# Attention of a mixer stage with keys and values expanded per head, head pairs in the two halves of TensorE, and the weights around it loaded earlier

## The chip, the cores and the metric

The kernel runs on one core of one Trainium2 chip. The metric is the device time of one execution in microseconds (us). Engine names are those of the profile: PE is TensorE, DVE is VectorE, ACT is ScalarE, SP is the engine that issues most DMAs.

## The reference

The program is a chain of blocks over 1024 tokens of width 1024. The change is in one of them, a mixer with sparse attention that runs between two feed-forward stages. Cut to what matters:

```
proj = h @ w_in                      # q (8 heads x 64), c (latent, 128), qi, ki, wi (index), z (gate, value)
c = rmsnorm(c)
q_abs = einsum('blhd,hcd->blhc', q, w_uk) * 64 ** -0.5
for each block of 128 queries:
    score = einsum(wi, relu(qi . ki));  score = where(causal, score, -inf)
    sel = top_k(score, 256)                           # the 256 keys that this query may see
    sc = q_abs . c[sel];  p = softmax(sc)             # 8 heads
    out = einsum('bqhc,hcd->bqhd', p @ c[sel], w_uv)
att, gmlp -> concatenated -> @ w_out -> deepnorm with the residual -> layernorm
```

The product q_abs . c equals q . (w_uk^T c), and (p @ c) @ w_uv equals p @ (c @ w_uv); either order may be used.

## The kernel before

The mixer stage (`mixer_stage`) has two parts, each a block of its own with a barrier behind it.

**Part "in_2"** computes `h @ w_in` in 16 tiles of 128 columns, each 48 matmuls of 512 columns in three fp32r products. Around the tiles it computes the index scores, the gated unit (`mix(n)`, eight matmuls whose outputs lie in alternating column halves, L2625) and the first steps of the selection. The threshold of the 256th score is found bit by bit, 64 rounds in all, 32 for blocks 2 to 4 and 32 for blocks 5 to 7. In one round (`rank_round`) DVE counts two blocks (L2498, twice), ACT the third (L2512), and DVE makes the next candidate (L2502, L2504). The table `ROUNDS_AFTER` puts 41 rounds into "in_2"; the other 23 are in the attention part, spread over its first 37 heads.

**Part "attention"** goes over 8 blocks of 128 queries and 8 heads, n = 8 b + h from 0 to 63. Block b sees k = b + 1 tiles of 128 keys. Its prologue transposes c (L2921) and makes q_abs per head (L2929, matmuls over 64 rows, alternating row halves); it waits for w_uk, w_uv and the mask, whose DMAs are issued as the part begins. For each n:

- PE: `score_head`, q_abs . c over 128 rows (L2887), k x 128 columns, into one of two halves of four PSUM banks.
- DVE: `add`, adds mask or selection and takes the row's maximum (L3051), then negates it (L3054).
- ACT: exponential with row sum (L2977).
- PE: k transposes (L2895); ACT copies them to SBUF, up to four tiles a copy (L2964).
- PE, once per pair of heads: `latent`, k matmuls of 256 columns (L2904); ACT copies (L2996); `value`, two matmuls of 64 columns (L2916).

Every engine's order is written out by hand; semaphores count the steps. PE does `score_head(n + 1)` ahead of the transposes of n. Once per block DVE scales the output by the inverse row sums (L3062, L3063), PE transposes it and ACT copies it to `mT`. Between heads DVE turns thresholds into a mask (`select`, L3011 to L3037) as a filler: `take(fill, ...)` runs its pieces up to a budget. `select(b)` must be done before the first head of block b.

After it `combine_stage("out_2", ...)` multiplies by `w_out`. Weights come through a ring of two slots (`Weights`): DMA into `ring_b_raw`, `cut_high` on ACT (L239), `cut_low` on DVE (L242). The part begins with the loads of its first two tiles (`primed` is False), then cuts `mT` in the same way, then multiplies.

Of the kernel before, what the change touches and what calls it, by code (L numbers as in the profile page):

```python
# [8 lines left out]
P = 128  # L9
D = 1024  # L10
KD = D // P
SEQ = 1024
CTX = 256
T = SEQ + CTX
DB = 512
# [9 lines left out]
NEG = -1.0e30  # L25
# [57 lines left out]
def program(nc, A):  # L83
# [18 lines left out]
    with root:  # L102
# [2336 lines left out]
        def mixer_stage(mT, ring, head):  # L2439
# [17 lines left out]
            MIX_AFTER = {13: (0, 1, 2), 14: (3, 4, 5), 15: (6, 7)}  # L2457
            MEAN_BANKS, VAR_BANKS, KV_BANKS = (6, 7), (2, 5), (6, 7)
            ROUNDS_AFTER = {3: 2, 4: 3, 5: 3, 6: 4, 7: 4, 8: 4, 9: 4, 10: 4, 11: 1, 12: 4, 13: 2, 14: 4, 15: 2}
# [4 lines left out]
                     "mix_ready", "a_loaded", "a_ctok", "a_ctok_ready", "a_qabs", "a_qabs_ready", "a_scored", "a_added",  # L2464
                     "rank_asked", "rank_told", "causal_added", "a_exp", "a_transposed", "a_turned", "a_latent", "a_latcopy", "a_value", "a_rescaled")
            S = {n: sem("att_" + n).h for n in names}

            with ExitStack() as mixer:
# [12 lines left out]
                links = []  # L2481
# [9 lines left out]
                def rank_round(link, dve, n):  # L2491

# [3 lines left out]
                    for i, b in enumerate(groups[g][:2]):  # L2496
                        w = (b + 1) * P
                        link(nc.vector.tensor_scalar(junk[:, 0:w], scores(b), cand[:, g, i:i + 1], float(TOPK - signed),  # L2498
                                                     ALU.is_ge, ALU.add, accum_out=found[:, g, i:i + 1]))
                    dve.wait_ge(S["rank_told"], n + 1)  # L2500
# [24 lines left out]
                with ExitStack() as ctx:  # L2525
# [29 lines left out]
                    with nc.Block("in_2") as block:  # L2555
                        @block.sync
                        def _(sp):
# [5 lines left out]
                            for m in range(n_tiles):  # L2563
                                if m >= 2:
                                    ring.load(sp, m // 2, m % 2, A["w_in"][tiles[m][1]])
                                if m == 2:
# [3 lines left out]
                                        .then_inc(S["mx_loaded"], 16)  # L2570

# [169 lines left out]
                        def _(dve):  # L2741
# [32 lines left out]
                            for m, _ in enumerate(steps):  # L2774
# [41 lines left out]
                                for _ in range(ROUNDS_AFTER.get(m, 0)):  # L2816
                                    rank_round(link, dve, ranked_here)
                                    ranked_here += 1
# [7 lines left out]
                qabs = sb(mixer, "at_qabs", [P, NH, SEQ])  # L2826
                ctok = sb(mixer, "at_ctok", [P, NQ, P])
                def uk(n):
                    return xT[:, n // 2, SEQ + n % 2 * P:SEQ + n % 2 * P + P]

                uv = sb(mixer, "at_uv", [P, NH, 64])
# [5 lines left out]
                sm = ring.raw[:, :].rearrange("p s k t -> p s (k t)")  # L2837
                pr = sb(mixer, "at_pr", [P, 2, SEQ])
                pT = sb(mixer, "at_pT", [P, 2, NQ, 2, P])
                mx = sb(mixer, "at_mx", [P, 2])  # L2840
                nmx = sb(mixer, "at_nmx", [P, 2])
                rs = sb(mixer, "at_rs", [P, 2, NH])
                lat = sb(mixer, "at_lat", [P, 2, 2, P])
                osb = sb(mixer, "att_rescaled_o", [P, 2, DB])
                N = NQ * NH
                PAIRS = N // 2
                STEPS = N + 7

                pieces, upto, out_at = [], {}, {}
                for n in range(STEPS):  # L2850
# [463 lines left out]
```

## Time and profile before

| | |
|---|---|
| median of 3 runs | 4023.18 us (4019.23 to 4026.61) |
| the profiled execution | 4014.95 us, its span 4013.2 us |
| granted TensorE clock, mean share of full | 0.958 |
| PE busy over the span | 3536.3 us (88%) |
| DVE, ACT busy over the span | 1917.4 us (48%), 1155.6 us (29%) |
| the attention part in the span | from 2862.8 to 3133.8 us |

A row of the view by windows gives the stretch, its length, then for PE, its weight loads, DVE, ACT and POOL the busy time and the count of instructions, then the granted clock (1.00 is 2.4 GHz, 0.50 is 1.2 GHz), DMA share and GB/s. A row of the timeline gives start, length, engine, line, operation, out<-in, shapes and count, and in brackets the idle time before it and what ended it. A row of the waits gives who waited for whom, the total, the times and the longest. A row of the groups gives busy time and mean ns of one, then idle time before. An fp32 matmul has two records in the trace.

### The profile page before, as it was taken

Reading aid. Unit: us, or ns where it says so; the run is one execution under the profiler, and the core shown is the slowest. Engines: PE = TensorE matmul, PEld = TensorE weight load, DVE = VectorE, ACT = ScalarE, POOL = GpSimd, SP = SyncE. Lnnn points to the kernel's source line nnn. Section 1 sums busy time; section 2 is a strip of 40 time slices with the busy share of each in tenths; the row PEclk is TensorE's granted clock in tenths of the full one; section 3 lists DMA queues with packets and bytes.
Section 4 is the critical chain, followed back from the end, with each engine's and each line's share of the span. In section 5 each row is a group of like instructions: output and inputs, shape, how many; then the busy total and the mean of one; then the engine's idle time right before and its main releaser. Section 6 shows DMA issues by size and latency. Waiting matters only on the chain. (4 is left out here: it accounts for less than half of the span.)

```text
span 4013.2 us, 67402 instructions
## 1 busy us (share of the span) xinstructions
PE 3536.3 (88%) x30218; PEld 2843.2 (71%) x30218; DVE 1917.4 (48%) x2775; ACT 1155.6 (29%) x1730; POOL 74.3 (2%) x85
## 2 busy tenths in 40 slices
PE   2999889998667777789999999999678889999997
PEld 1888678886256677647888888667456768888885
DVE  7555565643565565465222222657784552222226
ACT  2111231223434433333111111345364331111113
POOL 0000000000000000000000000110000020000000
PEclk9999999999789999989999999999799999999999
DMA  4233311223732222042111111210000211111112
GB/s 176 98 120 104 134 42 48 95 100 108 254 96 58 54 77 77 21 158 68 48 48 48 52 49 44 71 45 32 6 1 1 74 53 48 48 52 48 48 44 93
DMA packets 141796, 284.68 MB, mean 71 GB/s; under 512 B 8148, under 2 KB 81236, under 8 KB 141252
## 3 DMA queue, kind: packets, MB, share of 16 engines
q1 hardware_dynamic: 126212, 250.80, 19.4%
q10 hardware_dynamic: 15296, 29.57, 2.1%
q8 instruction: 238, 3.90, 0.4%
q14 instruction: 50, 0.41, 0.0%
HBM read 234.42 MB, written 45.65 MB: 70 GB/s over the span
## 5 line engine op out<-in xcount | busy, mean ns | idle before, releaser
L242 DVE TENSOR_TENSOR ring_b_wl<-ring_b_raw,ring_b_wh 128x1024 fp32r<-128x1024 f32 (+1 forms) x200 | 236.2, 1181 | 1115.2 <-ACT ring_b_wh L239 1115.2
L274 PE MATMUL PS<-ffn_x_high,ring_b_wh 128*128 128x512 f32 x1408 | 552.1, 392 | 11.0 <-DVE ffn_x_low L524 7.2
L276 PE MATMUL PS<-ffn_x_high,ring_b_wl 128*128 128x512 f32 x1408 | 549.8, 391 | 0.0
L275 PE MATMUL PS<-ffn_x_low,ring_b_wh 128*128 128x512 f32 x1408 | 549.8, 390 | 0.0
L239 ACT ACTIVATE ring_b_wh<-ring_b_raw 128x1024 fp32r<-128x1024 f32 (+1 forms) x200 | 204.6, 1025 | 1189.2 <-PE PS L276 1173.5
L274 PEld LDWEIGHTS PS<-ffn_x_high,ring_b_wh 128*128 128x128 f32 x1408 | 265.3, 188 | 72.8 <-DVE ffn_x_low L524 10.3
L276 PEld LDWEIGHTS PS<-ffn_x_high,ring_b_wl 128*128 128x128 f32 x1408 | 265.2, 188 | 55.2
L275 PEld LDWEIGHTS PS<-ffn_x_low,ring_b_wh 128*128 128x128 f32 x1408 | 265.4, 188 | 54.5 <-issue 0.2
L274 PE MATMUL PS<-ffn_hid_high,ring_b_wh 128*128 128x512 f32 x704 | 275.5, 391 | 2.6 <-DVE ring_b_wl L242 2.6
L276 PE MATMUL PS<-ffn_hid_high,ring_b_wl 128*128 128x512 f32 x704 | 274.4, 390 | 0.0
L275 PE MATMUL PS<-ffn_hid_low,ring_b_wh 128*128 128x512 f32 x704 | 274.3, 390 | 0.0
L242 DVE TENSOR_TENSOR ring_a_wl<-ring_a_raw,ring_a_wh 128x1024 fp32r<-128x1024 f32 x72 | 88.1, 1225 | 338.1 <-ACT ring_a_wh L239 337.8
L274 PE MATMUL PS<-in_o_high,ring_a_wh 128*128 128x512 f32 (+1 forms) x608 | 231.2, 380 | 10.9 <-DVE in_o_low L524 5.7
L239 ACT ACTIVATE ring_a_wh<-ring_a_raw 128x1024 fp32r<-128x1024 f32 x72 | 76.1, 1058 | 569.0 <-PE PS L276 545.0
L275 PE MATMUL PS<-in_o_low,ring_a_wh 128*128 128x512 f32 (+1 forms) x608 | 228.8, 376 | 0.0
L276 PE MATMUL PS<-in_o_high,ring_a_wl 128*128 128x512 f32 (+1 forms) x608 | 228.6, 376 | 0.0
L274 PE MATMUL PS<-in_e_high,ring_a_wh 128*128 128x512 f32 (+1 forms) x576 | 208.8, 363 | 14.4 <-DVE in_e_low L524 13.0
L275 PE MATMUL PS<-in_e_low,ring_a_wh 128*128 128x512 f32 (+1 forms) x576 | 205.0, 356 | 0.0
L276 PE MATMUL PS<-in_e_high,ring_a_wl 128*128 128x512 f32 (+1 forms) x576 | 204.9, 356 | 0.0
L274 PEld LDWEIGHTS PS<-ffn_hid_high,ring_b_wh 128*128 128x128 f32 x704 | 132.2, 188 | 32.2 <-DVE ring_b_wl L242 4.6
L275 PEld LDWEIGHTS PS<-ffn_hid_low,ring_b_wh 128*128 128x128 f32 x704 | 132.2, 188 | 27.8 <-issue 0.5
L276 PEld LDWEIGHTS PS<-ffn_hid_high,ring_b_wl 128*128 128x128 f32 x704 | 132.2, 188 | 27.3
(416 smaller groups left out, 6300.2 us busy)
## 6 DMA issues: line engine op xcount, KB each, us to landing
ring_b_raw<-in_ffn_up SPq DMA_DIRECT2D x88, 512.0 KB, 3.5
norm_e_t<-in_ada SPq DMA_DIRECT2D x32, 512.0 KB, 3.8
ring_a_raw<-in_in_o SPq DMA_DIRECT2D x32, 512.0 KB, 4.3
ring_b_raw<-in_ffn_down SPq DMA_DIRECT2D x32, 512.0 KB, 3.5
scan_tin<-scan_in SPq DMA_DIRECT2D x9, 1536.0 KB, 10.1
scan_in<-um SPq DMA_DIRECT2D x20, 641.0 KB, 9.5
ring_a_raw<-in_in_e SPq DMA_DIRECT2D x24, 512.0 KB, 3.6
ring_b_raw<-in_ffn_down SPq DMA_DIRECT2D x32, 384.0 KB, 3.1
```

Of the source, the lines that this page charges most:

```text
L239: return nc.scalar.activation(out, x, ACT.Copy)
L242: return nc.vector.tensor_tensor(out, x, high.bitcast(fp32), ALU.subtract)
L274: nc.tensor.matmul(out, wh, xh, start=k == 0, stop=False)
L275: nc.tensor.matmul(out, wh, xl, start=False, stop=False)
L276: last = nc.tensor.matmul(out, wl, xh, start=False, stop=k == kt - 1)
```

## The change

- `keys` = w_uk^T c per head and `vt` = c @ w_uv are made in the prologue; per pair of heads `score` then contracts over 64 rows, head 2j in rows 0 to 63 and head 2j + 1 in rows 64 to 127, and `value` multiplies the transposed probabilities by `vt` straight into the transposed output, the two heads in column halves. `latent`, its copy and the old `value` are gone, and so is the transpose of the output.
- The inverse sums are transposed and spread by a small matmul (`turn_inverse`, `spread_inverse`), once per block.
- Keys and mask are negated, so that the minimum is the bias as it stands and L3054 is gone.
- A round is split: `rank_ask` at one head, `rank_finish` at the next place that needs it. `ROUNDS_AFTER` has 4 rounds fewer (37), and `MIX_AFTER` ends one tile earlier.
- w_uk and w_uv are loaded into ring slot 0 during "in_2". The first two tiles of `w_out` are loaded and cut during the attention part, and "out_2" starts primed.

```diff
-            MIX_AFTER = {13: (0, 1, 2), 14: (3, 4, 5), 15: (6, 7)}
+            MIX_AFTER = {13: (0, 1, 2, 3), 14: (4, 5, 6, 7)}
-            ROUNDS_AFTER = {3: 2, 4: 3, 5: 3, 6: 4, 7: 4, 8: 4, 9: 4, 10: 4, 11: 1, 12: 4, 13: 2, 14: 4, 15: 2}
+            ROUNDS_AFTER = {3: 2, 4: 3, 5: 3, 6: 4, 7: 4, 8: 4, 9: 4, 10: 4, 11: 1, 12: 4, 13: 2, 14: 2}
@@ in_2, sync
+                            sp.wait_ge(w_low[0].h, w_low[0].base + n_tiles // 2)
+                            sp.dma_start(uk, A["w_uk"].rearrange("p h d -> p (h d)")).then_inc(S["a_weights"], 16)
+                            sp.dma_start(uv, A["w_uv"].rearrange("p h d -> p (h d)")).then_inc(S["a_weights"], 16)
@@ attention, sync
+                        sp.dma_start(causal[:, P:2 * P], A["neg"]).then_inc(S["a_loaded"], 16)
+                        sp.dma_start(xT[0:NH, 4:6, SEQ:T], A["heads_out"].rearrange("h (k j) t -> h k (j t)", k=2))\
+                            .then_inc(S["a_loaded"], 16)
+                        sp.wait_ge(S["a_keys"], NH // 2)
+                        load_following(ring, sp, 0, following)
@@ attention, tensor
+                        def score(p):
+                            b, j = p // 4, p % 4
+                            if 2 * p < NARROW:
+                                if p >= 2:
+                                    pe.wait_ge(S["a_added"], 2 * (p - 1))
+                            else:
+                                pe.wait_ge(S["a_added"], 2 * p)
+                            for c in range(0, (b + 1) * P, 512):
+                                w = min(512, (b + 1) * P - c)
+                                for i in range(2):
+                                    at, hp = row_at(2 * p + i) + c, slice(64 * i, 64 * i + 64)
+                                    last = nc.tensor.matmul(PS[:, at:at + w], mT[hp, j, b * P:b * P + P],
+                                                            keys[hp, j, c:c + w], start=True, stop=True)
+                            last.then_inc(S["a_scored"], 1)
+                        def value(p):
...
+                            for k in range(b + 1):
+                                for i in range(2):
+                                    last = nc.tensor.matmul(bank(6 + b % 2, P, j * P)[64 * i:64 * i + 64],
+                                                            vt[:, k, (2 * j + i) * 64:(2 * j + i) * 64 + 64],
+                                                            pT[:, p % 2, k, i, :], start=k == 0, stop=k == b,
+                                                            skip_group_check=True)
+                        for s in range(STEPS):
+                            if s + 1 < PAIRS:
+                                score(s + 1)
+                            if s < PAIRS:
+                                turn(2 * s)
+                                turn(2 * s + 1)
+                            if 0 <= s - 1 < PAIRS:
+                                value(s - 1)
+                            if s % 4 == 0 and s:
+                                turn_inverse(s // 4 - 1)
+                            if s % 4 == 1 and s > 1:
+                                spread_inverse(s // 4 - 1)
@@ attention, scalar
+                        for s in range(STEPS + 1):
+                            if 0 <= s - 1 < PAIRS:
+                                turned(2 * s - 2)
+                                turned(2 * s - 1)
...
+                            for n in (2 * s, 2 * s + 1):
+                                if n < N:
+                                    exponent(n)
                                 if n < len(ROUNDS_AT):
                                     for r in ROUNDS_AT[n]:
                                         sign_round(act, r)
+                            if s - PRIMED_FROM in (0, 1):
+                                ring.cut_high(act, 0, s - PRIMED_FROM)
@@ combine_stage("out_2"): primed False -> True
```

**PE, block 6** (k = 7; `at_cT` is c, `at_qabs` q_abs, `at_pr` the probabilities, `at_pT` their transposes, `at_ctok` c by tokens, `at_lat` the latent sum). One pair of heads before:

```order
L2887 MATMUL PS<-at_cT,at_qabs 128x512
L2887 MATMUL PS<-at_cT,at_qabs 128x384
L2895 MATMUL PS<-ident,at_pr 128x128 x7
L2904 MATMUL PS<-at_pT,at_ctok 128x256 x7
L2887 MATMUL PS<-at_cT,at_qabs 128x512
L2887 MATMUL PS<-at_cT,at_qabs 128x384
L2895 MATMUL PS<-ident,at_pr 128x128 x7
L2916 MATMUL PS<-at_uv,at_lat 128x64 x2
```

One pair of the same block now; L2911 is `score`, L2923 `turn`, L2933 `value`:

```order
L2911 MATMUL PS<-at_keys,mT 128x512 x2
L2911 MATMUL PS<-at_keys,mT 128x384 x2
L2923 MATMUL PS<-ident,at_pr 128x128 x14
L2933 MATMUL PS<-at_pT,at_values 64x128 x14
L2911 MATMUL PS<-at_keys,mT 128x512 x4
```

Scores of both heads stand together, all 14 transposes follow without other work between, and fourteen matmuls of 128 columns stand in the place of seven of 256 and two of 64. The last row is the score of the first pair of block 7.

**DVE, block 3**, one head with a round in it before, up to the next head's add:

```order
L3051 ISA ring_b_raw,at_mx<-PS,at_score 128x512
L3051 ISA at_mx 128x1
L3054 TENSOR_SCALAR at_nmx<-at_mx 128x1
L2498 TENSOR_SCALAR rank_junk,rank_found<-at_score,rank_cand 128x768
L2498 TENSOR_SCALAR rank_junk,rank_found<-at_score,rank_cand 128x896
L2502 TENSOR_SCALAR rank_back<-rank_found 128x3
L2504 SCALAR_TENSOR_TENSOR rank_cand<-rank_cand,rank_back 128x3
L3051 ISA ring_b_raw,at_mx<-PS,at_score 128x512
```

And now (L2499 is `rank_ask`, L2507 and L2509 `rank_finish`, L3099 the add):

```order
L3099 ISA at_rows,at_mn<-PS,at_score 128x512
L3099 ISA at_mn 128x1
L2507 TENSOR_SCALAR rank_back<-rank_found 128x3
L2509 SCALAR_TENSOR_TENSOR rank_cand<-rank_cand,rank_back 128x3
L2499 TENSOR_SCALAR rank_junk,rank_found<-at_score,rank_cand 128x768
L2499 TENSOR_SCALAR rank_junk,rank_found<-at_score,rank_cand 128x896
L3099 ISA at_rows,at_mn<-PS,at_score 128x512
```

The negation is gone, and the two small steps that need ACT's count stand behind the next add.

**DVE, end of "in_2" and start of the attention part.** Before (L2768 ends the last `scale_mix`):

```order
L2768 TENSOR_TENSOR mT<-mT,PS 128x4x128
L2498 TENSOR_SCALAR rank_junk,rank_found<-at_score,rank_cand 128x768
L2498 TENSOR_SCALAR rank_junk,rank_found<-at_score,rank_cand 128x896
L2502 TENSOR_SCALAR rank_back<-rank_found 128x3
L2504 SCALAR_TENSOR_TENSOR rank_cand<-rank_cand,rank_back 128x3
L2498 TENSOR_SCALAR rank_junk,rank_found<-at_score,rank_cand 128x768
L2498 TENSOR_SCALAR rank_junk,rank_found<-at_score,rank_cand 128x896
L2502 TENSOR_SCALAR rank_back<-rank_found 128x3
L2504 SCALAR_TENSOR_TENSOR rank_cand<-rank_cand,rank_back 128x3
L2555 UNCONDITIONAL_BRANCH
L2999 UNCONDITIONAL_BRANCH
L3068 MEMSET at_causal 128x128
```

Now the last two rounds stand behind tile 14, while PE multiplies tile 15, and nothing follows on DVE. These rows begin with the last instruction of "in_2":

```order
L2509 SCALAR_TENSOR_TENSOR rank_cand<-rank_cand,rank_back 128x3
L2560 UNCONDITIONAL_BRANCH
L3041 UNCONDITIONAL_BRANCH
L3115 MEMSET at_causal 128x128
L3116 MEMSET at_one_row 128x1024
L3119 COPY at_values<-PS 128x512 x8
```

Two rounds behind the last tile are gone, and eight copies of values stand ahead of the first selection.

## Rows read from the trace of the kernel before

**Rows 1.** View by windows: stages of the attention part, start of "out_2".

```profile
2862.80:2883.70 20.90, 15.07 (x44) 6.72 (x44) 10.10 (x19) 8.44 (x9) 0.00 (x0) 0.79 0.09 29
2883.70:3010.00 126.30, 95.87 (x420) 66.58 (x420) 108.39 (x300) 77.66 (x196) 0.00 (x0) 0.88 0.00 1
...
3047.00:3084.90 37.90, 34.62 (x165) 25.12 (x163) 10.91 (x27) 17.99 (x37) 0.00 (x0) 0.95 0.00 1
3084.90:3133.80 48.90, 43.13 (x209) 31.39 (x207) 12.78 (x28) 21.76 (x41) 0.00 (x0) 0.97 0.00 1
3133.80:3141.80 8.00, 0.00 (x0) 0.00 (x1) 3.17 (x4) 4.09 (x6) 0.00 (x0) 0.55 0.49 150
```

**Rows 2.** DVE's waits from 2883.7 to 3010, the longest.

```profile
DVE ring_b_raw L3051 <- PE PS L2887: 14.0, 10, 5.1
DVE at_rs L3062 <- PE PS L2916: 1.2, 2, 0.9
```

**Rows 3.** DVE's waits from 3047 to 3133.8, the longest.

```profile
DVE ring_b_raw L3051 <- PE PS L2887: 54.7, 16, 5.5
```

**Rows 4.** Timeline across the barrier between "in_2" and attention, PE and DVE.

```profile
2851.24 1.03 PE L2615 MATMUL PS<-ident,gmlp_v 128*128 128x128 f32 x8
...
2862.11 0.16 DVE L2504 SCALAR_TENSOR_TENSOR rank_cand<-rank_cand,rank_back 128x3 int32<-128x3 int32 x1
...
2862.80 1.52 PE L2921 MATMUL PS<-ident,at_cT 128*128 128x128 f32 x6 [7.83 <-PEq L2555]
...
2867.97 3.79 PE L2929 MATMUL PS<-mT,xT 64*128 64x512 f32 x8 [3.22 <-DMA at_causal<-in_neg]
```

**Rows 5.** Timeline of DVE in block 3: one head with a round.

```profile
2950.94 0.08 DVE L3051 DVE_READ_ACCUMULATOR2_ANT at_mx<- 128x1 f32 x1
2951.05 0.15 DVE L3054 TENSOR_SCALAR at_nmx<-at_mx 128x1 f32<-128x1 f32 x1
2951.19 1.01 DVE L2498 TENSOR_SCALAR_CACHE_REDUCE rank_junk<-at_score,rank_cand 128x768 uint8<-128x768 f32 x1
...
2953.84 0.69 DVE L3051 CUSTOM_DVE_ANT_0 ring_b_raw<-PS,at_score 128x512 f32<-128x512 f32 x1
```

**Rows 6.** Timeline of PE in block 6: one pair of heads.

```profile
3062.11 1.67 PE L2887 MATMUL PS<-at_cT,at_qabs 128*128 128x512 f32 x4
3063.61 0.93 PE L2895 MATMUL PS<-ident,at_pr 128*128 128x128 f32 x7
...
3067.69 3.19 PE L2904 MATMUL PS<-at_pT,at_ctok 128*128 128x256 f32 x14
3070.71 1.67 PE L2887 MATMUL PS<-at_cT,at_qabs 128*128 128x512 f32 x4
```

**Rows 7.** Timeline of PE: column halves (L2625) and row halves (L2929).

```profile
2810.98 1.09 PE L2625 MATMUL PS<-xT 128*64 128x128 f32 x16 [1.73 <-ACT xT L2700]
2812.01 0.66 PE L2615 MATMUL PS<-ident,gmlp_v 128*128 128x128 f32 x4
2812.59 1.09 PE L2625 MATMUL PS<-xT 128*64 128x128 f32 x16
...
2872.85 2.90 PE L2929 MATMUL PS<-mT,xT 64*128 64x512 f32 x8 [1.10 <-ACT at_qabs L2955]
```

**Rows 8.** Groups of ACT in the attention part, by form.

```profile
L2964 ACT ACTIVATE at_pT<-PS 128x512 f32<-128x512 f32 x48 | 26.9, 577 | 0.1
L2977 ACT ACTIVATE at_pr<-ring_b_raw,at_nmx 128x1024 f32<-128x1024 f32 x8 | 9.2, 1148 | 17.5 <-DVE at_nmx L3054 17.5
```

**Rows 9.** Timeline of DVE: last filler ahead of head 0, head 0, head 44.

```profile
2877.88 0.75 DVE L3035 SCALAR_TENSOR_TENSOR at_score<-at_score,rank_cand,at_work 128x512 f32<-128x512 f32 x1
2883.69 0.29 DVE L3051 CUSTOM_DVE_ANT_0 ring_b_raw<-PS,at_causal 128x128 f32<-128x128 f32 x1 [5.05 <-PE PS L2887]
...
3029.27 0.96 DVE L3051 CUSTOM_DVE_ANT_0 ring_b_raw<-PS,at_score 128x768 f32<-128x768 f32 x1
```

**Rows 10.** Timeline of the start of "out_2".

```profile
3141.00 1.89 DVE L242 TENSOR_TENSOR out_low<-mT,out_high 128x512 fp32r<-128x512 f32 x3
```

More of the change, by code:

```diff
@@ L2436, in ffn_stage, with mixer_stage @@
                 totals.end()
[L2439 removed]
+        def mixer_stage(mT, ring, head, following):
             NQ, NH = SEQ // P, 8
@@ L2909, in value @@
-                        def value(p):
-                            b = 2 * p // NH
-                            pe.wait_ge(S["a_latcopy"], p + 1)
-                            if 2 * p % NH == 0 and b:
-                                pe.wait_ge(S["a_rescaled"], b)
-                            for i in range(2):
-                                h = (2 * p + i) % NH
-                                last = nc.tensor.matmul(bank(7, 64, h * 64), lat[:, p % 2, i, :], uv[:, h, :], start=True,
-                                                        stop=True)
-                            last.then_inc(S["a_value"], 1)
@@ new lines, in turn_inverse, with spread_inverse @@
+                        def turn_inverse(b):
+                            t = place["turned", b, 0]
+                            pe.wait_ge(S["a_inverse"], b + 1)
+                            pe.wait_ge(S["a_turned"], t - 1)
+                            nc.tensor.transpose(bank(4 + t % 2, P)[0:NH], rs[:, b % 2, :], ident[:, :])\
+                                .then_inc(S["a_transposed"], 1)
+                        def spread_inverse(b):
+                            t = place["spread", b, 0]
+                            pe.wait_ge(S["a_turned"], max(t - 1, place["turned", b, 0] + 1))
+                            for j in range(NH // 2):
+                                last = nc.tensor.matmul(bank(4 + t % 2, P, j * P), heads_out(j), rT[:, :], start=True, stop=True)
+                            last.then_inc(S["a_transposed"], 1)
@@ L2960, in turned @@
                             if p >= 2:
-                                act.wait_ge(S["a_latent"], p - 1)
-                            for t, k0, count in steps_of(n):
+                                act.wait_ge(S["a_value"], p - 1)
+                            for k0 in range(0, n // NH + 1, 4):
+                                t, count = place["head", n, k0], min(4, n // NH + 1 - k0)
                                 act.wait_ge(S["a_transposed"], t + 1)
```

288 lines of the change are left out of this document (144 added, 144 removed).

## Prediction

> **What bounds the kernel now.** I began with the windows, because the change touches one stage of ten. The attention part runs from 2862.8 to 3133.8, 271 of the 4013 us, and it isn't bounded by one engine. From 2883.7 to 3010 (heads 0 to 39) DVE is busy for 108.4 of 126.3 us; its waits for scores come to 14.0, of which 5.05 lie ahead of the first add, so 9.0 lie inside [rows 1, 2, 9]. Most of the rest is the 0.03 between one of its instructions and the next [rows 5]. DVE is the chain there. From 3047 to 3133.8 it's reversed: DVE waits 54.7 us for PE's scores and is busy for 24 of 87, while PE is busy for 78 [rows 1, 3]. Between them (3010 to 3047) DVE still has selections until head 44 at 3029.27 [rows 9], and PE after that.
>
> Around it lie three stretches in which PE multiplies little or nothing. The last product of "in_2" is over at 2851.24, DVE works on rounds until 2862.27, and PE starts the next block at 2862.80; then it waits for DMAs until 2867.97 [rows 4]. The prologue as a whole takes 20.9 us. And from 3133.8 to 3141.8 PE does nothing at all, since the first weights of "out_2" are loaded and cut first [rows 1, 10].
>
> **End of "in_2".** Two rounds behind the last tile go, and two more behind tile 14; mixing moves ahead of the last tile. On PE the last product starts later: two mixes of 1.1 us each (eight matmuls, [rows 7]) with their transposes move in front of it, and they wait for one another through DVE; I take 3 us. Its end moves from 2851.2 to 2854.3. ACT's evacuation (1024 columns; 1.0, below the 1.15 of an exponential of that width, [rows 8]) and the barrier (0.5, as from 2862.27 to 2862.80) put the new block at 2856.0: **6.8 us** earlier. It can't be over 11.
>
> **Prologue.** The weights are in SBUF, so the 5.2 us of waiting go. PE now makes 8 matmuls of 512 columns for values and 8 for keys. 896 columns take 1.50 us [rows 6], so 512 take 0.855, and the sixteen take 13.7. The copy of the last keys (again 1.0 to 1.15) and the first score bring head 0 to 15.6. On DVE eight copies of 512 columns (0.69 each, as the add of that width, [rows 5], so they keep up with PE) end at about 7.7. Then the filler of before follows: it has two selections, which end at 2878.63 [rows 9] and can't have begun before 2867.97 [rows 4] and a memset and a copy of about 2.3 behind that; 8.3: 16.3 in all. Head 0 starts at 2872.3, not 2883.7, **4.6 us** gained beside the 6.8.
>
> **Heads 0 to 39.** DVE's own work lies between its busy 108.4 and 116.1, which is 126.3 less the two waits of rows 2; with 0.03 behind some 180 of its 300 instructions I take 113.9. L3054 goes: 0.14 from its start to the next [rows 5], 40 times, minus 5.6. Four more rounds come in: one takes 2951.19 to 2953.84, 2.65 us [rows 5], plus 10.6. Deferring `rank_finish` costs DVE nothing, and ACT's count (one pass over 1024 elements, like the exponential's 1.15) fits under DVE's own two and the next add. I leave 2.5 us for waits, since `score` now runs a whole pair ahead and the first four blocks have four row slots. Sum 121.4, against 126.3: **4.9 us**. Head 40 is at 2993.7. Bounds: no wait at all 119; the old 12.4 (126.3 less 113.9) again 131.
>
> **Heads 40 to 63.** First DVE has its selections: from head 40 to head 44 3009.97 to 3029.27, 19.3; without four negations and the rescale, which comes later, 17.8. So the score of the third pair of block 5 ends at about 3012.9. Then PE's loop sets the pace. In step s it does score(s + 1), turn(2s), turn(2s + 1), value(s - 1). With k key tiles:
>
> - score: two heads of 128 k columns in the two row halves. L2929 shows four matmuls of 512 columns over 64 rows in 2.90 us, where one behind another is 3.42, and the second pair of them waited for ACT for the first 0.9 [rows 7]. So the halves run side by side at full rate, and a pair costs one head's columns, 0.214 k.
> - turn: 0.11 per transpose (seven in 0.93, eight in 1.03, [rows 4, 6]). But with k over 4 the second head's first chunk needs the bank of the first head's, and ACT copies that only after both exponentials. So PE waits: four transposes with their latency 0.65, the copy 0.58 [rows 8], two semaphores 0.12, together 1.35; then 0.11 k for the second head.
> - value: 2 k matmuls of 128 columns in column halves. L2625 shows eight in 1.03 with a switch to transposes behind them, 0.11 each [rows 7], where 128 columns alone take 0.214. So 0.22 k.
> - switches between whole array and halves: four transposes occupy 0.58 up to the next start, not 0.44 [rows 7]; 0.15 each, three in a loop, 0.45.
>
> The loop is 1.8 + 0.544 k: 5.1, 5.6 and 6.15 us for k = 6, 7, 8. One pair of block 6 now takes 3062.11 to 3070.71, 8.6 us [rows 6]. ACT needs less than the loop (under 2.5 for two exponentials, under 2.3 for four copies, [rows 8]), DVE too: an add is 0.69 for 512 columns and 0.96 for 768 [rows 5, 9], two for 896 make 2.4 with their reads. From the score at 3012.9: two loops of 5.1, four of 5.6, three of 6.15 make 51.1; the inverse (one transpose, four small matmuls, two switches) 1.5 in each of two blocks; cutting the primed weights 1. The last score ends at 3068.0. The tail behind it has the last two turns, two values, the inverse, its copies and the rescale, one behind another: 4.3 + 1.35 + 0.9 + 1.7 + 1.75 + 4.4 = 14.4. End 3082.4; from head 40 that is 88.7, against 123.8: **35.1 us**.
>
> A rule of the Trainium skill speaks against this part: TensorEngine Tiling (Array Packing), Key Properties, says that changing the tiling mode drains TensorE. The trace agrees in kind, with the 0.14 above. It would turn the sum over only if a drain cost much more than it does there.
>
> **"out_2".** Its operand cut starts with the block. The first low part, now at 3141.00, 7.2 us behind 3133.8 [rows 10], needs only a high part first: about 1. **6.2 us** gained. The two DMAs are issued in the prologue and have 150 us.
>
> **Sum.** 6.8 + 4.6 + 4.9 + 35.1 + 6.2 = 57.6 us. The profiled execution took 4014.95 around its span of 4013.2, and would come to 3957; the median of the runs lies 8.2 above it. I take the difference off the median: **3966 us**.
>
> **The rivals.**
> - *The halves don't overlap in this mix.* Rows 7 have one kind of matmul in a row; here a pair alternates between kinds. Score and value would each double, 0.434 k more a loop; over the nine loops and the tail (k sums to about 70) 30 us: 3996. The rows speak against it. Chance 0.12.
> - *PE is granted 1.2 GHz in the last blocks*, because it streams half the columns and waits for ACT once a loop. Blocks 6 and 7 now have 0.95 and 0.97, the first 126 us 0.88 [rows 1]. At half rate throughout a loop would grow by 0.544 k + 0.7, some 4.5; if half of the eleven loops suffer, 25 us: 3991. Chance 0.10. The Trainium skill, TensorE: Matmul & The Clock Gate, Part 4, says that a transpose doesn't count as activity of TensorE in the way a matmul does; by that this case would be likelier, as transposes are now a larger share of the loop.
> - *ACT or DVE, not PE, is shorter than I think*: the wait for a copy is partly covered and DVE never waits. Loops of 4.8 and 5.2, ACT's own, give 6 us, DVE's bound 2.5, "in_2" 2: 3955. Chance 0.18.
> - *Slower.* The split round: if ACT's count is late, DVE stands at `rank_finish` in each of 27 rounds. ACT's queue has two copies, each waiting for PE's transposes, ahead of the two exponentials and the counts of a step, and PE's turn stands behind a score that waits for DVE's adds. It needs 57.6 / 27 = 2.1 us a round to eat the gain; at 2.6, 4036. I work it out for k = 5: copies 1.2, exponentials 1.8 and two counts 2.6 make 5.6 on ACT against 7 on DVE, so there is slack. Chance 0.03.
> - *Little is gained*: a new wait in the wide blocks (adds of a pair before the next score) of 4 us a loop, 4016. Chance 0.02.
>
> **Range.** The forecast has 0.55, its own range 3958 to 3978 (waits 119 to 124 in DVE's part, 0.5 us a loop either way). With the rivals on either side, and the first one's and the clock's 3991 to 3996 mostly inside, the range is 3948 to 3998. Of faster by over 0.2% (8 us, about what a measurement of this kernel can tell from no change), within it, and slower I expect 0.95, 0.02 and 0.03.
>
> **What would show it.** Attention starts 6 to 7 us behind the last product of "in_2" less than before, with no wait for a DMA. DVE in heads 0 to 39 busy over 91%, rounds of 2.65 and no wait at L2507. In block 6 scores of a pair (1792 columns) within 1.6 us, fourteen value matmuls in 1.6 to 1.7, one wait of PE for a copy by ACT per pair, and a period of 5.6. "out_2" multiplying within 2 us. Wrong would be: a period over 6.5 at k = 7, a clock under 0.9 from head 40 on, or waits of DVE for ACT over 5 us in sum.

## The result, and the profile after

The changed kernel takes 3969.24 us (median of 4 runs, 3966.88 to 3971.45), the kernel before 4022.7 (4 runs, 4019.23 to 4026.61). The ratio is 0.9867, with a 95% interval of 0.9856 to 0.9879. The forecast was 3966, with 3948 to 3998 as its range.

The two profiled spans, 4013.2 and 3969.6, are only 43.6 us apart. That is 10 us less than the medians, since the profiled execution of before was one of the quick ones: it reaches the start of "in_2" at 2589.8, while in the profiles of the changed kernel and its eleven variants here this start lies at 2594 to 2602, although nothing ahead of it was changed. The profiled execution of the changed kernel was the slowest of its four. So I compare stretches counted from the start of "in_2" (the first cut of its operand). From there to the first matmul of "out_2" it was 552.1 us before, and is 501.2 now: 50.9 us less. What lies behind it is 871.3 and 869.2 us.

The windows of the changed kernel: the prologue, heads 0 to 39, block 5, block 6, block 7 to the end of attention, and from there to the first matmul of "out_2".

```profile
2862.20:2878.60 16.40, 14.69 (x40) 6.55 (x40) 14.53 (x27) 5.38 (x5) 0.00 (x0) 1.00 0.10 26
2878.60:3005.60 127.00, 86.42 (x447) 51.24 (x447) 110.30 (x283) 76.43 (x187) 0.00 (x0) 0.65 0.02 6
3005.60:3038.80 33.20, 23.10 (x171) 15.25 (x172) 21.59 (x38) 15.03 (x34) 0.00 (x0) 0.85 0.00 1
3038.80:3063.00 24.20, 21.95 (x200) 15.18 (x201) 9.26 (x19) 16.54 (x34) 0.00 (x0) 1.00 0.00 1
3063.00:3098.60 35.60, 29.43 (x304) 22.31 (x304) 13.47 (x22) 23.06 (x42) 0.00 (x0) 1.00 0.01 2
3098.60:3100.40 1.80, 0.00 (x0) 0.02 (x1) 0.83 (x3) 1.49 (x3) 0.00 (x0) 1.00 0.21 36
```

Beside [rows 1]: the prologue went from 20.9 to 16.3 us, heads 0 to 39 from 126.3 to 127.0 although four more rounds lie in it, blocks 6 and 7 from 86.8 to 59.8, and the empty 8.0 ahead of "out_2" to 1.8. The granted clock fell in heads 0 to 39 (0.65, before 0.88) and in block 5 (0.85, before 1.00 from 3010 to 3047), and rose in blocks 6 and 7 (1.00, before 0.95 and 0.97).

DVE's waits in heads 0 to 39, which answer to [rows 2]:

```profile
DVE rank_back L2507 <- ACT rank_signs L2517: 8.6, 6, 3.8
DVE rank_junk L2499 <- DVE rank_cand L2509: 4.2, 26, 0.2
```

There is no wait for PE's scores left, where there were 9.0 us. The new wait is the one for ACT's count, 8.6 us in six pieces. The second row is no stall to remove: it is 0.16 between two dependent instructions of each round.

DVE's waits in blocks 6 and 7 (3038 to 3098), which answer to [rows 3], and PE's in the same stretch:

```profile
DVE at_rows L3099 <- PE PS L2911: 18.3, 6, 4.0
```

```profile
PE PS L2923 <- ACT at_pT L2997: 6.5, 9, 1.5
```

DVE's 54.7 us of waiting for scores have become 18.3. It waits there for ACT too, 13.1 us for copies of the spread inverses, of which 7.5 stand in the tail, and 7.9 us for the high parts of w_out's tiles. PE itself waits for 6.9 of the 60 us, so from block 6 on it still sets the pace, together with ACT's copies.

The timeline across the barrier, which answers to [rows 4]:

```profile
2860.93 1.02 ACT L2694 ACTIVATE mT<-PS 128x1024 f32<-128x1024 f32 x1 [5.88 <-PE PS L276]
2862.26 1.95 PE L2957 MATMUL PS<-ring_b_raw,at_cT 128*128 128x512 f32 x4 [1.37 <-PEq L2560]
2862.32 0.17 DVE L3115 MEMSET at_causal<- 128x128 f32 x1 [5.82 <-PEq L2560]
```

PE starts the new block 1.4 us behind the last product (11.6 before, 2851.24 to 2862.80), and multiplies at once.

DVE in block 3, from one `rank_finish` to the next add, as [rows 5]:

```profile
2945.46 0.16 DVE L2507 TENSOR_SCALAR rank_back<-rank_found 128x3 int32<-128x3 f32 x1
...
2945.99 1.01 DVE L2499 TENSOR_SCALAR_CACHE_REDUCE rank_junk<-at_score,rank_cand 128x768 uint8<-128x768 f32 x1 [0.16 <-DVE rank_cand L2509]
...
2948.23 0.69 DVE L3099 CUSTOM_DVE_ANT_0 at_rows<-PS,at_score 128x512 f32<-128x512 f32 x1
```

A round with nothing late costs 2.77 us, for the 2.65 that I took. And one pair of heads on PE in block 6, as [rows 6]:

```profile
3055.02 1.77 PE L2911 MATMUL PS<-at_keys,mT 64*128 64x512 f32 x8
3056.79 0.98 PE L2923 MATMUL PS<-ident,at_pr 128*128 128x128 f32 x7
3058.39 0.96 PE L2923 MATMUL PS<-ident,at_pr 128*128 128x128 f32 x7 [0.61 <-ACT at_pT L2997]
3059.28 1.75 PE L2933 MATMUL PS<-at_pT,at_values 128*64 128x128 f32 x28
3060.96 0.70 PE L2911 MATMUL PS<-at_keys,mT 64*128 64x512 f32 x2
```

Scores of 1792 columns take 1.77 us and fourteen value matmuls (28 records) 1.75, so both kinds of halves run side by side. PE waits once for ACT's copy. The pair takes 5.94 us (8.6 before, [rows 6]). From add to add the four pairs of block 6 take 5.4, 5.75, 6.9 and 6.1, with the inverse in them; the block took 37.8 before and takes 24.2.

### The profile page after: what moved, and what is told of

It reads as the page before. It is cut to its first block and busy times, and to the rows that moved or that the text cites. A ratio compares the mean times of both kernels' runs of the same rounds, so it can differ in the third digit from the quotient of the medians.

```text
span 3969.6 us, 67614 instructions
## 1 busy us (share of the span) xinstructions
PE 3495.1 (88%) x30410; PEld 2805.9 (71%) x30410; DVE 1909.7 (48%) x2719; ACT 1144.3 (29%) x1702; POOL 74.7 (2%) x85
## 5 line engine op out<-in xcount | busy, mean ns | idle before, releaser
L274 PE MATMUL PS<-in_o_high,ring_a_wh 128*128 128x512 f32 (+1 forms) x608 | 230.3, 379 | 11.6 <-DVE in_o_low L524 6.5
L274 PE MATMUL PS<-in_e_high,ring_a_wh 128*128 128x512 f32 (+1 forms) x576 | 208.5, 362 | 14.4 <-DVE in_e_low L524 13.1
## 6 DMA issues: line engine op xcount, KB each, us to landing
scan_in<-um SPq DMA_DIRECT2D x20, 641.0 KB, 10.6
```

Of the source, the lines that this page charges most:

```text
L274: nc.tensor.matmul(out, wh, xh, start=k == 0, stop=False)
```

## The experiments

All times below stand against two references: the changed kernel's 3969.24 above, and a second measurement of it unchanged, beside the first experiments.

**The changed kernel once more.**

> The changed kernel once more, beside the three that alter one place of it. All theories: 3969 us, 53 to 54 us under the kernel before; in the trace the stretch from head 0 to head 40 takes 126 to 128 us, with 7 to 10 us of waits of DVE for ACT's count.

3971.64 us (3969.23 to 3976.03), ratio 0.9878. The kernel before took 4019.25 beside it, so the gain is 47.6 us here and 53.5 in the first measurement; I had expected 53 to 54 again. Its stretches: prologue 16.3, heads 0 to 39 127.4, from head 40 to the end of attention 92.0, sum from "in_2" 502.9. They repeat within 1 us, except one: attention starts 263 us behind the start of "in_2" in four of the thirteen profiles of the changed kernel and its variants, and 265 to 266 in the others, whatever was edited. The two kinds of profile part early in "in_2", which none of the edits touches. Here are 8 us from 28 us behind its start on, of the changed kernel (263) and of the one without primed weights below (265.4):

```profile
2627.17:2635.17 8.00, 5.48 (x21) 3.25 (x19) 5.66 (x8) 3.31 (x5) 8.00 (x6) 1.00 0.00 0
```

```profile
2626.91:2634.91 8.00, 6.79 (x16) 4.21 (x15) 5.48 (x7) 2.57 (x4) 8.00 (x6) 0.58 0.00 0
```

The granted clock is 1.00 in this stretch in the four profiles at 263, and 0.58 to 0.84 in the nine others. The profile of the kernel before has 0.59 and belongs with the nine. Why the clock dips in one execution and not in another stays open.

So differences of 2 us in the sum mean nothing; those of one stretch do, if they are larger than the 1 us by which it repeats here (1.6 in one pair of profiles below). Behind the first matmul of "out_2" unchanged code takes 868.8 to 873.6 us. Among the medians of such variants I read nothing under 7 us, since three kernels whose stretches otherwise agree with the first measurement's within 2 us (this one and two below) lie 2 to 7 us above it.

**Four more rounds in "in_2"** (41 there, as before).

```diff
-ROUNDS_AFTER = {3: 2, 4: 3, 5: 3, 6: 4, 7: 4, 8: 4, 9: 4, 10: 4, 11: 1, 12: 4, 13: 2, 14: 2}
+ROUNDS_AFTER = {3: 2, 4: 3, 5: 3, 6: 4, 7: 4, 8: 4, 9: 4, 10: 4, 11: 1, 12: 4, 13: 4, 14: 4}
```

> Two more rounds of the selection behind tile 13 and two more behind tile 14 of in_2 (41 there, 23 in attention). Theory: DVE is idle for 7.5 and 5.8 us at these places and is the chain from head 0 to 40, so four rounds of 2.65 us vanish from the path: 9 to 11 us less than control, heads 0 to 39 in about 116 us, attention begins at the same place. Rival: that stretch is set by ACT's queue behind PE at the low clock, not by DVE's work; then under 4 us.

3963.65 us (3961.41 to 3964.73), ratio 0.986 [0.9845, 0.9874]. Heads 0 to 39 take 116.8 for 127.0:

```profile
2876.39:2993.22 116.83, 74.89 (x447) 44.54 (x447) 100.36 (x260) 72.02 (x180) 0.00 (x0) 0.75 0.02 7
```

DVE's busy time falls by 9.9 us, which is the four rounds, and attention starts no later than in most profiles (265.7 behind the start of "in_2"). The barrier takes 0.3 us more (1.7 from the end of the last product, not 1.4). DVE stands idle for 7.46 us ahead of `mix(4)` and for 5.8 us during the last product, so these rounds fit there. The change had moved work from where it cost at most 0.3 us to where it cost 10.

**The spread copy behind the exponentials.** At the first pairs of a block ACT copies the spread inverses (L3021), ahead of two exponentials and two counts.

```diff
-    if (s - 1) % 4 == 1 and s > 2:
-        inverse_spread((s - 1) // 4 - 1)
     for n in (2 * s, 2 * s + 1):
...
+    if (s - 1) % 4 == 1 and s > 2:
+        inverse_spread((s - 1) // 4 - 1)
```

The longest wait of the changed kernel shows why. All engines, in order of time:

```profile
2926.39 2.07 PE L2950 MATMUL PS<-at_rT,xT 8*128 8x128 f32 x8
...
2928.50 0.60 ACT L3021 ACTIVATE xT<-PS 128x512 f32<-128x512 f32 x1 [2.93 <-PE PS L2950]
...
2929.59 1.14 ACT L2517 ACTIVATE rank_signs<-at_score,rank_cand 128x1024 int8<-128x1024 f32 x1
...
2930.85 0.17 DVE L2507 TENSOR_SCALAR rank_back<-rank_found 128x3 int32<-128x3 f32 x1 [3.83 <-ACT rank_signs L2517]
```

ACT waits 2.93 us for PE's spread, PE makes it behind the values and at half clock, and DVE's count comes 3.83 us late. Four of the six waits, 6.7 of the 8.6 us, end 2.3 to 2.7 us behind the start of such a copy.

> ACT copies the spread inverse sums behind the exponentials and counts of its step, not ahead of them. Theory: the single wait of 3.8 us at the split round comes from that copy, which waits for PE's small matmuls; it and the smaller ones of the same place go, 4 us less than control, waits of DVE for ACT's count under 5 us. Rival: ACT is late for other reasons (copies of the transposes), then within 1.5 us of control.

3963.64 us (3957.28 to 3964.43), ratio 0.9857 [0.9842, 0.9872]. Heads 0 to 39 take 121.8, the rest 90.8 (93.0). The same place now, ACT and DVE:

```profile
2926.09 1.14 ACT L2517 ACTIVATE rank_signs<-at_score,rank_cand 128x1024 int8<-128x1024 f32 x1
...
2927.23 0.58 ACT L3021 ACTIVATE xT<-PS 128x512 f32<-128x512 f32 x1
...
2929.48 0.16 DVE L2507 TENSOR_SCALAR rank_back<-rank_found 128x3 int32<-128x3 f32 x1
```

No wait stands there. The waits for ACT's count sum to 3.4 us in two pieces: 5.2 less, and the stretch is shorter by 5.2. So this order is the cause of most of what the first 40 heads lost against the forecast (127.0 for 121.4).

**`rank_finish` right behind `rank_ask`**, as in the kernel before.

```diff
-    finish_round()
     rank_ask(link, r)
-    open_rounds.append(r)
+    rank_finish(link, dve, r)
```

> A round's second half directly behind its first, as before the change; all else as changed. Theory: with ACT working by pairs its count is often 1 to 3 us late, so 27 rounds now wait, 10 to 30 us more than the changed kernel. Rival: ACT is in time; then 3 us less, since the 0.16 between one round's end and the next round's beginning is paid less often.

3982.78 us (3980.32 to 3986.93), ratio 0.9898 [0.9883, 0.9913]. Heads 0 to 39 take 137.8, and the waits for the count grow to 22.0 us:

```profile
DVE rank_back L2507 <- ACT rank_signs L2517: 22.0, 8, 4.7
```

Splitting the round is worth 10.8 us with the rest as it is. I take it to be needed because everything now goes by pairs, so ACT's queue holds two exponentials and two counts at once; that isn't tested. Four of the eight waits, 13.4 of the 22.0 us, again end 2.4 to 2.8 us behind the start of a spread copy. What the split is worth once that copy stands late, no run shows.

**More work for PE in blocks 0 to 4**, to test whether the lower clock there matters. 4 or 6 matmuls of 128 columns a pair go to the values' place in PSUM, which the values then overwrite.

```diff
+    for _ in range((4, 4, 6, 6, 6, 0, 0, 0)[b]):
+        nc.tensor.matmul(bank(6 + b % 2, P, j * P), ident[:, :], cT[:, 0:P], start=True,
+                     stop=True, skip_group_check=True)
```

> Adds 4 to 6 matmuls of 128 columns, whose result is overwritten, ahead of each pair's value in blocks 0 to 4 (no part of the result changes). Theory: from head 0 to 40 PE's clock was granted at 0.65, and its slow small matmuls make ACT late for DVE; with more work the clock stays above 0.85, DVE's waits for ACT's count fall from 8.6 to under 4 us, 2 to 5 us less than the changed kernel. Rival: the clock costs nothing there since DVE sets the pace; same time, or a few us more for the added work.

3981.63 us (3980.48 to 3982.91), ratio 0.9894 [0.988, 0.9909]. The clock of the stretch rises from 0.65 to 0.82, and the stretch is 7.6 us longer, where I had expected 2 to 5 less:

```profile
2877.84:3012.44 134.60, 95.71 (x631) 69.75 (x631) 110.47 (x284) 76.32 (x187) 0.00 (x0) 0.82 0.02 7
```

The waits for the count are 15.6 us in place of 8.6: the added matmuls stand ahead of PE's next transposes, and these ahead of ACT's copies. Up to head 24 the clock rises from 0.54 to 0.83 and the time stays (59.4 and 59.6 us); the loss is all behind it. What a full clock alone would give isn't shown by this, since the added work costs too. At this price it isn't worth having.

**Values head by head** in place of alternating halves.

```diff
-    for k in range(b + 1):
-        for i in range(2):
+    for i in range(2):
+        for k in range(b + 1):
             last = nc.tensor.matmul(bank(6 + b % 2, P, j * P)[64 * i:64 * i + 64],
...
```

> The value matmuls of a pair in the order of heads: all of the first head (one column half), then all of the second. Same matmuls. Theory (alternating halves run side by side): they now run one after another, 0.2 k us a pair; over the pairs in which PE sets the pace (k sums to about 80) 14 to 18 us more than the changed kernel, and the 14 matmuls of a pair in block 6 take 3.0 us, not 1.7. Rival (the halves didn't overlap anyway): no change.

3992.86 us (3986.82 to 3994.84), ratio 0.9924 [0.9907, 0.994]. The row of PE that was 1.75 us:

```profile
3058.80 2.89 PE L2933 MATMUL PS<-at_pT,at_values 128*64 128x128 f32 x28
```

From head 40 on it takes 105.3 for 93.0, heads 0 to 39 131.5 for 127.0. By the stretches the alternating order of the column halves carries 17 us of the kernel's gain (by the medians 21 to 24), and the two kernels do the same matmuls. But 2.89 isn't twice 1.75: a part still overlaps.

**Scores head by head.**

```diff
-    for c in range(0, (b + 1) * P, 512):
-        w = min(512, (b + 1) * P - c)
-        for i in range(2):
+    for i in range(2):
+        for c in range(0, (b + 1) * P, 512):
+            w = min(512, (b + 1) * P - c)
```

> The score matmuls of a pair in the order of heads: both chunks of the first head (rows 0 to 63), then of the second. Theory: as above, 14 to 18 us more, a pair of block 6 takes 3.0 us for its scores instead of 1.6. Milder form: the second head's matmuls begin while the first head's last one streams, so that little more than half of it is seen, 8 to 12 us. Rival: no change.

3976.47 us (3971.79 to 3979.56), ratio 0.988 [0.9866, 0.9895]. From head 0 on every stretch is that of the changed kernel within 0.1 us (127.0 and 93.1), and so is the row:

```profile
3059.62 1.78 PE L2911 MATMUL PS<-at_keys,mT 64*128 64x512 f32 x8
```

I had expected a loss here as for the values. There was none, and a theory was missing. The single records gave one. With values by head the second head's first matmul started at 3059.954, together with the first head's sixth of seven (3059.948): it stood two places behind it. With scores by head there are only two matmuls a head, so the second head's first stands two places behind the first head's first, and starts with it.

**How far a matmul of the other half may stand behind.** Scores head by head with four chunks a head, and values in runs of two.

```diff
-    for c in range(0, (b + 1) * P, 512):
-        w = min(512, (b + 1) * P - c)
-        for i in range(2):
+    for i in range(2):
+        for c in range(0, (b + 1) * P, 256):
+            w = min(256, (b + 1) * P - c)
...
-    for k in range(b + 1):
-        for i in range(2):
+    for k, i in [(k, i) for k0 in range(0, b + 1, 2) for i in range(2)
+                 for k in range(k0, min(k0 + 2, b + 1))]:
```

> Two edits that the trace keeps apart. The transposed values go in runs of two (two matmuls of one column half, two of the other); the scores go head by head in chunks of 256 columns, four chunks a head in place of two. Theory A: TensorE starts a matmul on the idle half when it stands no more than about two places behind the one that runs, whichever kind of half it is. In the run with values by head the second head's first pass began when two of the first head's seven matmuls were left, and scores by head had only two matmuls a head, so nothing was lost. By it the value block of a pair stays at 1.75 us for k = 7 (up to 1.95), and the score of a pair goes from 1.77 to about 2.5, since two of the first head's four chunks (0.43 each) run alone; the period of a pair in block 6 grows by 0.6 to 0.9 and the kernel takes 4 to 10 us more than the changed one. Theory B: row halves overlap in any order and column halves only where they alternate strictly. By it the score stays at 1.8, values rise to 2.3 or more for k = 7, and the kernel takes 5 to 10 us more. If both stay as they are, the reach is four matmuls or more, and the time is that of the changed kernel.

3988.76 us (3981.32 to 3991.96), ratio 0.9914 [0.9898, 0.993]. Scores and values for k = 7:

```profile
3060.31 2.75 PE L2911 MATMUL PS<-at_keys,mT 64*128 64x256 f32 x16
...
3065.38 1.80 PE L2934 MATMUL PS<-at_pT,at_values 128*64 128x128 f32 x28
```

Values stay at 1.8, scores go from 1.77 to 2.75. One of the scores in single records: the first head's four chunks start at 3053.531, 3054.067, 3054.497 and 3054.929, the second head's first at 3054.503, with the third. Two places behind again. So it's no matter of rows or columns: theory A holds for both kinds. Theory B, by which only columns needed the right order, falls. What in TensorE sets this reach isn't shown. The medians are 17 to 20 us more where I had expected 4 to 10. By the stretches it is 11.6: the period of a pair grows by 1.0 in block 6 (24.2 to 28.1), head 40 to the first matmul of "out_2" loses 7.2 in all, and heads 0 to 39 lose 4.4 as well, which I hadn't counted.

**Both primed cuts behind the last head.** In the changed kernel ACT cuts w_out's tiles between the copies of block 7:

```profile
3075.77 1.04 ACT L239 ACTIVATE ring_b_wh<-ring_b_raw 128x1024 fp32r<-128x1024 f32 x1
3076.72 1.05 ACT L2997 ACTIVATE at_pT<-PS 128x512 f32<-128x512 f32 x2
...
3077.43 1.06 PE L2923 MATMUL PS<-ident,at_pr 128*128 128x128 f32 x8 [1.19 <-ACT at_pT L2997]
```

PE waits for the copy behind the cut, and two pairs take 9.0 and 8.5 us.

```diff
-    if s - PRIMED_FROM in (0, 1):
-        ring.cut_high(act, 0, s - PRIMED_FROM)
+    if s == PAIRS:
+        for m in range(2):
+            ring.cut_high(act, 0, m)
```

and the same for `cut_low` on DVE.

> Both primed weight tiles are cut in the tail, when the last exponentials are done, and not at pairs 29 and 30. Theory: each cut lies on the chain of block 7, where PE waits 1.2 and 1.5 us for a copy instead of 0.4 and DVE's next add is late; 2 to 4 us less than control, the periods of block 7 fall from 8 to 9 us to 6.2 to 7.5. Rival: the tail has no room, the cuts end behind the attention part and out_2 starts later; 0 to 2 us more.

3975.05 us (3967.5 to 3977.81), ratio 0.9886 [0.9871, 0.99]. The pairs take 6.3 and 7.4, and head 40 to the end 91.2 for 93.0. So 1.8 us locally, a little under the 2 to 4 expected. The time of the whole shows nothing of it: its median lies 3 to 6 us above the changed kernel's, within what I don't read. The cuts now stand in the tail:

```profile
3090.67 2.01 ACT L239 ACTIVATE ring_b_wh<-ring_b_raw 128x1024 fp32r<-128x1024 f32 x2
```

They don't lengthen it. From the end of the last score to the end of attention it's 14.2 us, as in the kernel without any cut below (14.1), and 15.2 in the changed kernel, whose second cut starts behind the last score. The rival, a tail without room, falls.

**"out_2" not primed.** The load and both cuts in attention are left out, and "out_2" begins with them.

```diff
-    load_following(ring, sp, 0, following)
...
-    if s - PRIMED_FROM in (0, 1):
-        ring.cut_high(act, 0, s - PRIMED_FROM)
...
-combine_stage("out_2", ring, A["w_out"], mT, MAIN_CHUNKS, BY_CHUNK, deepnorm_update, False, ln2, True, A["ffn2_up"])
+combine_stage("out_2", ring, A["w_out"], mT, MAIN_CHUNKS, BY_CHUNK, deepnorm_update, False, ln2, False, A["ffn2_up"])
```

> The changed kernel without the early load and cuts of the first two tiles of w_out: the first cut of out_2 is again an operand that waits for its DMA. Theory: the stretch between attention and the first matmul of out_2 goes from 1.8 back to 8.0 us (+6.2), and block 7 loses the two waits that the cuts make, pairs of 9.0 and 8.5 going back to about 6.3 and 7.4, 3.8 us; but as with the cuts moved behind the last head, only 1 to 2 us of it reach the end, since the score of the next pair is ahead. So 4 to 5 us slower than the changed kernel locally, 3972 to 3977. Rival: the cuts cost as much as they bring, and the time is the changed kernel's within 2 us locally.

3984.49 us (3981.55 to 3990.16), ratio 0.9908 [0.9893, 0.9923]. From the end of attention to the first matmul it's 8.1 us, not 1.8, and ACT's first cut waits for the DMA again:

```profile
3102.59 1.06 ACT L239 ACTIVATE ring_b_wh<-ring_b_raw 128x1024 fp32r<-128x1024 f32 x1 [4.59 <-DMA ring_b_raw<-in_w_out]
```

From head 40 to the end of attention it's 1.9 us less (91.1). The net is 4.4 us by the stretches, as expected. The medians differ by 13 to 15, outside the 3972 to 3977 expected and more than any stretch shows. In the two profiles 2.3 lie in "in_2", where the clock dips in one of them and 4.4 lie behind the first matmul of "out_2" (873.6 for 869.2), where the changed kernel's own second measurement has 872.6; the rest I can't place.

**Putting them together.** Four more rounds in "in_2", the spread copy late and the cuts moved:

> Three edits together on the changed kernel: four more rounds behind tiles 13 and 14 (none of them left for the wide heads), the copy of the spread inverse behind the exponentials of its step, and both primed cuts behind the last head. Alone they gained locally 8 to 10, 7 and 1 to 2 us. The first two shorten the same stretch of heads 0 to 39 (127.0 to 116.8 and to 121.8), where DVE's own work is 106 to 110, so they can't add up fully: I expect 113 to 115 there, 90.5 for the rest, the local sum at 488 to 491, 10 to 13 us below the changed kernel, 3956 to 3960. Rival: the waits that the first removes are the ones that the second removes, and both give no more than the first alone, 3963.

3959.44 us (3956.72 to 3960.14), ratio 0.9842 [0.9829, 0.9856]. Heads 0 to 39 take 111.0 and the rest 90.0. And without the moved cuts:

> The same without the moved cuts: four more rounds behind tiles 13 and 14 and the spread copy behind the exponentials. If the moved cuts are worth the 1.8 us that they gave locally, this takes 1 to 2 us more than the kernel with all three; if what they gave is within the measurement, both times agree within 2 us. Heads 0 to 39 113 to 115, the rest 91 to 92.5.

3955.21 us (3954.38 to 3956.66), ratio 0.9833 [0.9819, 0.9846]. That is 14 us below the changed kernel. Its windows for heads 0 to 39 and from there to the end of attention, and the wait for the count:

```profile
2880.43:2993.00 112.57, 76.03 (x447) 45.36 (x447) 100.23 (x259) 72.41 (x178) 0.00 (x0) 0.72 0.02 7
2993.00:3083.80 90.80, 72.29 (x675) 51.46 (x673) 44.33 (x78) 54.90 (x110) 0.00 (x0) 0.96 0.01 1
```

```profile
DVE rank_back L2507 <- ACT rank_signs L2517: 2.1, 3, 1.5
```

The two edits that had given 10.2 and 5.2 in heads 0 to 39 give 14.4 together (112.6, a little below the 113 to 115 that I had expected): they nearly add up, so the rival by which they remove the same wait falls. A new wait appears: DVE waits 3.1 us for the spread copy before it rescales (1.7 with the four rounds alone, none with the late copy alone or in the changed kernel).

Whether moving the cuts is worth doing these two runs don't tell. By the stretches the kernel with moved cuts is 1.8 us shorter (485.2 and 487.0), but only 0.8 of it lies from head 40 on (91.8 and 92.6 to the first matmul of "out_2"); 1.6 lies in heads 0 to 39 (111.0 and 112.6), where the two kernels are alike, so that stretch repeats no better than that. By the medians it takes 4 more, of which 3.7 stand behind the first matmul of "out_2" (873.0 and 869.3).

## Why the prediction was right, and where not

The time came out 3 us above the forecast, inside the likeliest case's own 3958 to 3978, and in the main by the mechanism that was forecast. The medians differ by 53.5 us, for the 57.6 of the sum; the stretches, counted from the start of "in_2", show 50.9, and 2.1 more lie behind the first matmul of "out_2", where unchanged code scatters by more than that. So the sum was too large by 7, with misses of both signs in it. That the time lies so near is in part luck. The kernel before was profiled with the clock's dip in "in_2" and the changed one without; like with like that part is worth 7.5 and the sum 48.5, near the 47.6 of the second pair of medians.

| step | predicted | measured |
|---|---|---|
| "in_2" and barrier | 6.8 | 9.9 here, 7.5 against profiles with the same dip |
| prologue | 4.6 | 4.6 |
| heads 0 to 39 | 4.9 | -0.7 |
| head 40 to the end | 35.1 | 30.8 |
| start of "out_2" | 6.2 | 6.2 |
| sum | 57.6 | 50.9 |

**"in_2".** Right in kind. The last product ends 0 to 3 us later (I took 3), and the barrier costs 1.4 us behind it, where evacuation and barrier together were to take about 1.7.

**Prologue.** Right to the tenth: 16.3, with no wait for a DMA and head 0 held by the two selections, as worked out.

**Heads 0 to 39: the step that failed.** DVE's own part was right: I had 113.9 - 5.6 + 10.6 = 118.9, and 127.0 less 8.6 of waiting is 118.4. The wrong sentence is "ACT's count fits under DVE's own two and the next add. I leave 2.5 us for waits". It was 8.6. I had worked out ACT's load for a pair and compared it with DVE's, and on average it fits. What I left out is the spread copy, which stands once per block at the head of ACT's queue and waits for the last thing PE does in a step. The late copy took 5.2 of it away. And the sum took the four rounds as given. They cost 10.2 us here and nothing in "in_2".

**Head 40 to the end.** Right in kind: halves side by side, one wait for a copy a pair and, in blocks 6 and 7, a clock of 1.00. Three terms were too small, 4.3 us in all. The largest is the loop. The pair above took 5.94 us, not 5.6: its scores 1.77 for the 1.50 put, the first head's transposes up to the second's 1.60 for 1.35. In the kernel without the cuts the nine loops and two inverses took 56.8 us from the score of the third pair of block 5 to the last score, for 54.1. Then that third pair: DVE reached head 44 after 17.8 us, as put, but waited 2.52 us more for a score (eight records) that took 2.93 us at a granted clock of 0.50, so the score ended 20.2 us behind head 40 and not 19.2. And "cutting the primed weights 1" was 1.8 to 1.9: 3.8 in the pairs of block 7, of which 0.8 reached the last score, and 1.1 behind it. The tail without a cut in it took 14.1, for 14.4.

**"out_2".** Right: 1.8 us to the first matmul, from 8.0.

**The rivals.** *The halves don't overlap*: no, but the experiments show that this rival was a matter of order. With the values by head it costs 17 us, over half of the 30 that I had for values and scores together. *1.2 GHz in the last blocks*: no, 1.00 there. The low clock came instead in heads 0 to 23, at 0.54, and again in parts of block 5 (0.85 over the block). Most of it fell where DVE is the bound; it lengthened the spread and the score of heads 44 and 45. The Trainium skill, TensorE: Matmul & The Clock Gate, Part 4, says of TensorE's transpose mode that it doesn't count as busy in the way a matmul does. The loops of blocks 6 and 7 hold two transposed heads a pair and still show 1.00, so by these rows the share of transposes there didn't matter. *Slower, by the split round*: its mechanism was the one that acted, at 8.6 / 27 = 0.3 us a round, a seventh of the 2.1 needed to eat the gain. *Shorter loops* and *little gained* didn't happen.

Of the signs that the prediction named, some came out against it: DVE was busy for 87% of heads 0 to 39, not over 91; its waits for ACT, which were to be wrong above 5 us, came to 8.6; and the clock, which was not to fall under 0.9 from head 40 on, was 0.94 over all of it but 0.85 in block 5.

The Trainium skill's rule on draining, TensorEngine Tiling (Array Packing), Key Properties, didn't turn the sum over: from transposes to values a start is 0.89 behind for seven transposes (3058.39 to 3059.28 above), where seven at 0.11 are 0.77. That is 0.12 us a switch, near the 0.14 of the kernel before. The same section says that different tiles can execute matmuls in parallel; the trace agrees for both kinds of halves, but only for matmuls that stand near each other in the queue.

## What to carry to other kernels

Where an in-order queue holds a count or a copy that another engine waits for, don't ask whether its load fits on average; ask what stands directly ahead of it and what that itself waits for. One copy per block at the head of ACT's queue, waiting for the last product of a step, cost 5.2 us, more than the 3.4 that all other waits for the count in 27 rounds came to. Before moving filler out of a stage, look for idle time left in that stage: four rounds cost at most 0.3 us in "in_2" and 10 us in attention. The fp32 matmuls for two halves of TensorE ran best here written alternately, or in runs of at most two.

## What the runs showed of the hardware that I had not expected

- A matmul on the idle half started with the matmul two places ahead of it, and no sooner: values in runs of seven 2.89 us, in runs of two 1.80, alternating 1.75; scores in runs of four 2.75, in runs of two 1.78, alternating 1.77. Rows and columns behave alike.
- The granted clock fell to 0.50 and stayed low in a stretch that PE entered at full clock, where its short matmuls have gaps between them (42.2 us busy of 59.4, 0.54). With more matmuls in it the same stretch was granted 0.83 and ended no earlier.
- Attention starts either 263 or about 265.5 us behind the start of "in_2", from profile to profile, with no edit to go with it. The profiles differ in the granted clock 28 to 36 us behind that start, 1.00 in the first kind and 0.58 to 0.84 in the second. Behind the first matmul of "out_2" the changed kernel's two profiles have PE busy for 836.7 and 840.0 us with the same 3604 records, and the stretch takes 869.2 and 872.6.
